# A decoder block on one core: x turned unscaled, its row factors applied at the PSUM copies, and the bias row's matmuls at the front

## The reference

```python
def rmsnorm(x, g):
    xf = x.astype(jnp.float32)
    y = xf * lax.rsqrt(jnp.mean(xf * xf, axis=-1, keepdims=True) + EPS)
    return (y * g.astype(jnp.float32)).astype(x.dtype)

h = rmsnorm(x, g_mix[layer])
proj = h @ w_in[layer]                       # (512, 1024) @ (1024, 5632)
q, k, v, u, gate_a, gate_s = jnp.split(proj, SPLITS, axis=-1)
attn = diff_attention(q, k, v, rel_bias, lam, subln_g[layer], lam_init)   # 8 heads, two softmaxes each, T5 bias
y = s5_ssm(u, ...)                           # 32 groups of 16 channels, 64 complex states
z_val, z_gate = jnp.split(jax.nn.gelu(y) @ w_glu[layer], 2, axis=-1)
mixed = jax.nn.sigmoid(gate_a) * attn + jax.nn.sigmoid(gate_s) * (z_val * jax.nn.sigmoid(z_gate))
x = x + mixed @ w_out[layer]
h = rmsnorm(x, g_mlp[layer])
x = x + jnp.square(jax.nn.relu(h @ w1[layer])) @ w2[layer]
return rmsnorm(x, g_final)
```

## Time and profile before

| | us |
|---|---|
| median of 3 timed runs | 774.8 |
| lowest, highest | 773.28, 776.76 |
| the profiled execution's own time | 769.86 |
| its span (first to last instruction) | 768.1 |
| TensorE busy in it | 747.2 (97%) |
| VectorE (DVE) busy | 529.9 (69%) |
| ScalarE (ACT) busy | 359.5 (47%) |
| GpSimd (POOL) busy | 29.2 (4%) |

### The profile page before, as it was taken

How to read it: one execution, slowest core, us unless ns; L and a number is a source line. 1 busy time by engine, 2 the same in 40 slices (tenths; PEclk the granted TensorE clock), 3 DMA queues, 4 the chain that set the end, 5 groups by cost and what they waited for, 6 DMA issues and landing times.

```text
span 768.1 us, 10026 instructions
## 1 busy us (share of the span) xinstructions
PE 747.2 (97%) x3754; PEld 611.2 (80%) x3754; DVE 529.9 (69%) x951; ACT 359.5 (47%) x630; POOL 29.2 (4%) x28
## 2 busy tenths in 40 slices
PE   6999999999999999999999999999999999999995
PEld 5878878777777777888878787888888888888884
DVE  4679998655556673436742578866886498748896
ACT  7524631255556663732322645533543345334454
POOL 2210000000000100000000000000000000000015
PEclk9999999999999999999999999999999999999998
DMA  7673429922223530236237131183108320743002
GB/s 245 195 164 117 103 94 183 219 72 70 69 69 108 168 110 2 84 108 247 83 110 192 55 101 37 52 225 108 55 1 231 126 83 0 191 139 91 19 2 109
DMA packets 91824, 85.21 MB, mean 111 GB/s; under 512 B 10028, under 2 KB 68064, under 8 KB 91776
## 3 DMA queue, kind: packets, MB, share of 16 engines
q1 hardware_dynamic: 90944, 82.85, 38.4%
q10 hardware_dynamic: 832, 1.71, 1.1%
HBM read 77.11 MB, written 5.34 MB: 107 GB/s over the span
## 4 chain that ended last, share of the span: by engine, by line
PE 75%; DVE 16%; ACT 3%; issue 3%; DMA 2%; SPq 1%; DVEq 0%; ACTq 0%
PE ps L1649 22%; PE ps L1651 22%; PE ps L1650 22%; PE ps L1940 3%; PE ps L1921 3%; DVE w_lo L1008 2%; DMA raw<-in_w_in 1%; PE ps L1930 1%; DMA mixA<-in_x 1%; PE ps L1724 1%; DVE w_lo L1412 1%; DVE fr L1425 1%; DVE rt L1257 1%; DVE mixA L1383 1%; ACT fa_hi L880 1%
## 5 line engine op out<-in xcount | busy, mean ns | idle before, releaser
L1649 PE MATMUL ps<-hT_hi,w_hi 128*128 128x512 f32 x384 | 152.6, 397 | 0.4 <-DVE hT_lo L980 0.3
L1651 PE MATMUL ps<-hT_hi,w_lo 128*128 128x512 f32 x384 | 150.1, 391 | 0.0
L1650 PE MATMUL ps<-hT_lo,w_hi 128*128 128x512 f32 x384 | 149.7, 390 | 0.0
L1649 PE MATMUL ps<-w_hi,hT_hi 128*128 128x512 f32 x288 | 114.3, 397 | 0.0
L1651 PE MATMUL ps<-w_hi,hT_lo 128*128 128x512 f32 x288 | 112.4, 390 | 0.0
L1650 PE MATMUL ps<-w_lo,hT_hi 128*128 128x512 f32 x288 | 112.3, 390 | 0.0
L847 ACT ACTIVATE w_hi<-raw 128x1024 fp32r<-128x1024 f32 x78 | 81.7, 1052 | 56.4 <-PE ps L1651 56.4
L1412 DVE TENSOR_TENSOR w_lo<-raw,w_hi 128x1024 fp32r<-128x1024 f32 x78 | 94.2, 1221 | 15.6 <-ACT w_hi L847 14.7
L613 ACT ACTIVATE w_hi<-raw 128x1024 fp32r<-128x1024 f32 x62 | 64.8, 1058 | 68.5 <-PE ps L1651 58.3
L1008 DVE TENSOR_TENSOR w_lo<-raw,w_hi 128x1024 fp32r<-128x1024 f32 x58 | 70.4, 1222 | 32.4 <-ACT w_hi L613 31.8
L1649 PE MATMUL ps<-w_hi,fa_hi 128*128 128x512 f32 x224 | 87.4, 390 | 1.4 <-DVE fa_lo L1435 1.2
(11 more groups left out here) (256 smaller groups left out, 996.0 us busy)
## 6 DMA issues: line engine op xcount, KB each, us to landing
raw<-in_w SPq DMA_DIRECT2D x64, 512.0 KB, 4.3
raw<-in_w_in SPq DMA_DIRECT2D x44, 512.0 KB, 5.1
raw<-in_w_glu SPq DMA_DIRECT2D x8, 512.0 KB, 3.9
raw<-in_w_out SPq DMA_DIRECT2D x8, 512.0 KB, 4.0
mixA<-in_x SPq DMA_DIRECT2D x4, 512.0 KB, 5.4
bias<-frow_dram SPq DMA_DIRECT2D x32, 64.0 KB, 2.0
toep<-taps_dram SPq DMA_DIRECT2D x8, 256.0 KB, 9.6
x<-in_x SPq DMA_DIRECT2D x4, 512.0 KB, 6.7
```

What stands on the lines that cost most here:

```text
L1649: nc.tensor.matmul(dst, a_hi, b_hi, start=start, stop=False)
L1650: nc.tensor.matmul(dst, a_hi, b_lo, start=False, stop=False)
L1651: return nc.tensor.matmul(dst, a_lo, b_hi, start=False, stop=stop)
```

## The change

- SP issues `rb` and `oneh` first of all; then row tiles 0 to 2 of x, weight unit 0, row tile 3, and units 1 to 3.
- TensorE does the two bias matmuls as its very first work, and DVE their copies. `bias_row` behind `turn_prm` is gone, and so are DVE's two copies behind `mag`.
- TensorE turns x as it lands, unscaled. Tile 3 comes last with all its eight blocks; column 7 of tiles 0 to 2 is turned before it.
- ACT squares tiles 0 and 1 before the split of unit 0, and tiles 2 and 3 after the last `turn_hi`; one root and one reciprocal serve all four tiles.
- `w_lo` of unit 0 moves from GpSimd to DVE, in two halves, around the first `turn_lo`. TensorE does the u unit 0 column by column (all four row tiles for k = 0, then for k = 1).
- The row factor (`rstd`) comes in where ACT copies u, V and the gates (as the activation's scale). For q and k the tokens lie along the free axis: SP writes the four columns of `rstd` to DRAM (four DMAs of 128 x 4 bytes, in front of the load of unit 4) and reads them back spread over all partitions (`rows0`, 128 x 512, behind the taps' store). `copy_qk` moves from ACT to DVE as a scalar_tensor_tensor with `rows0` as second operand.
- In DVE's program `copy_qk(0)` stands behind `gate_a(0)`, `copy_qk(1)` behind the w_lo of unit 22 and in front of `gate_a(1)`, and the others at the end of each pair.

```diff
@@ SP
-        for t in range(TOK):
+        sp.dma_start(rb[:, :], rel_bias).then_inc(onehot_in, 16)
+        sp.dma_start(oneh[:, :], onehot).then_inc(onehot_in, 16)
...
-        for u in range(RING):
+        for t in range(TOK - 1):
+            load_x(t)
+        load_raw(0)
+        load_x(TOK - 1)
+        for u in range(1, RING):
             load_raw(u)
...
+        sp.wait_ge(x_rstd, TOK)
+        for t in range(TOK):
+            sp.dma_start(rstd_dram[P * t:P * t + P].unsqueeze(1), rstd[:, 0, t:t + 1]).then_inc(rstd_out, 16)
+
+        def load_rows0():
+            sp.wait_ge(taps_mm, 1)
...
+            sp.dma_start(rows0[:, :], bass.AP(rstd_dram.tensor, 0, [[0, P], [1, SEQ]])).then_inc(rows0_in, 16)
@@ ACT
+        square_x(0)
+        square_x(1)
         act.wait_ge(cols_turned, 1)
...
         for k in range(KT):
             turn_hi(0, k, g1_col)
-            if k == 2:
+            if k == 3:
                 split_hi(1)
+        square_x(2)
+        square_x(3)
+        act.wait_ge(x_squared, TOK)
+        nc.scalar.activation(ms[:, 0, 1, :], ms[:, 0, 0, :], ACT.Sqrt, bias=eps_t[:, :],
+                             scale=1.0 / D_MODEL).then_inc(x_rt, TOK)
...
-                                             ACT.Identity).then_inc(nat_copied, 1)
+                                             ACT.Identity, scale=rstd[:, 0, t:t + 1]).then_inc(nat_copied, 1)
@@ DVE
+        dve.wait_ge(frow_mm, 1)
+        TS(frow[:, 0:512], ps[0:N_HEADS, 5, :], 1.0, None, ALU.mult).then_inc(frow_out, 1)
...
+        split_first(0)
         dve.wait_ge(cols_copied, 1)
-        for k in range(KT):
+        turn_lo(0, 0, g1_col)
+        split_first(1)
+        for k in range(1, KT):
             turn_lo(0, k, g1_col)
...
+        def copy_qk(v):
+            h = v // 2
+            if v == 0:
+                dve.wait_ge(states_done, 2)
+                dve.wait_ge(frow_done, 16)
+                dve.wait_ge(rows0_in, 16)
+            dve.wait_ge(unit_used, U_QK + v + 1)
+            if h >= 2:
+                dve.wait_ge(score_ready, TOK * (h - 1))
+            dst, src = (qT, kT)[v % 2][:, h % 2, :], ps[:, qk_bank(v), :]
+            STT(out=dst, in0=src, scalar=HEAD_DIM ** -0.5 if v % 2 == 0 else 1.0, in1=rows0[:, :],
+                op0=ALU.mult, op1=ALU.mult).then_inc(qk_copied, 1)
+
         split_lo_to(U_QK + 2)
         gate_a(0)
+        copy_qk(0)
         split_lo_to(U_QK + 3)
+        copy_qk(1)
         gate_a(1)
         split_lo_to(U_QK + 4)
...
             if i == 0 and h >= 1:
                 gate_o(h - 1)
+            if h < N_HEADS - 1:
+                copy_qk(2 * (h + 1) + i // 2)
@@ TensorE
+        pe.wait_ge(onehot_in, 32)
+        nc.tensor.matmul(ps[0:N_HEADS, 5, :], rb[:, :], oneh[:, 0:512], start=True, stop=True)
...
         for t in range(TOK):
-            pe.wait_ge(x_scaled, t + 1)
-            for k in range(KT - 1):
+            pe.wait_ge(x_in[t], 16)
+            for k in (0, 3, 4, 5, 6, 1, 2) if t == 0 else range(KT) if t == TOK - 1 else range(KT - 1):
...
+        for k in range(2):
+            if k:
+                pe.wait_ge(w_lo_done, 1)
+            else:
+                pe.wait_ge(w0_part, 1)
+            for t in range(TOK):
+                pe.wait_ge(hT_lo_done, max(t, k) + 1)
+                mm = drive_input(U_SSM, t, k)
+        unit_done(mm)
```

More of the change, by code:

```diff
@@ L177, in build @@
     y_sb = sb("y_sb", [P, CHUNK, PAIRS, SSM_GROUP], offset=at["CL"])
+    rows0 = sb("rows0", [P, SEQ], offset=at["CL"] + 16384)
     y_nat = sb("y_nat", [P, TOK, SSM_WIDTH], offset=at["u_nat"])
@@ L550, in _ @@
         nc.gpsimd.memset(powers[:, 0, 1, :], 0.0).then_inc(tiles_set, 1)
-        for u in range(U_V):
+        pool.wait_ge(w_lo_done, 1)
+        for u in range(1, U_V):
             pool.wait_ge(w_hi_done, u + 1)
@@ L595, in _, with square_x @@
             act.dma_start(dst, src).then_inc(cols_in, 16)
-        for t in range(TOK):
+        def square_x(t):
             act.wait_ge(x_in[t], 16)
@@ L982, in turn_lo, with split_first @@
             ins.then_inc(hT_lo_done, 1)
-        for t in range(TOK):
-            dve.wait_ge(x_rt, t + 1)
-            nc.vector.reciprocal(rstd[:, 0, t:t + 1], ms[:, 0, 1, t:t + 1]).then_inc(x_rstd, 1)
-            dve.wait_ge(x_rstd, t + 1)
-            TS(mixA[:, t, :], mixA[:, t, :], rstd[:, 0, t:t + 1], None, ALU.mult).then_inc(x_scaled, 1)
+        dve.wait_ge(frow_mm, 1)
+        TS(frow[:, 0:512], ps[0:N_HEADS, 5, :], 1.0, None, ALU.mult).then_inc(frow_out, 1)
+        TS(frow[:, 512:BIAS_W], ps[0:N_HEADS, 6, 0:BIAS_W - 512], 0.0, MASKED, ALU.mult, ALU.add).then_inc(frow_out, 1)
+        def split_first(half):
+            cs = slice(512 * half, 512 * half + 512)
+            dve.wait_ge(w_hi_done, 1)
+            TT(w_lo[:, 0, cs], raw[:, 0, cs], w_hi[:, 0, cs].bitcast(F32),
+               ALU.subtract).then_inc(w_lo_done if half else w0_part, 1)
+        split_first(0)
         dve.wait_ge(cols_copied, 1)
-        for k in range(KT):
+        turn_lo(0, 0, g1_col)
+        split_first(1)
+        for k in range(1, KT):
             turn_lo(0, k, g1_col)
+        dve.wait_ge(x_rt, TOK)
+        nc.vector.reciprocal(rstd[:, 0, :], ms[:, 0, 1, :]).then_inc(x_rstd, TOK - 1)
+        dve.wait_ge(x_rstd, TOK - 1)
+        TS(rstd[:, 1, :], rstd[:, 0, :], 0.5, None, ALU.mult).then_inc(x_rstd, 1)
         def prow(i):
@@ L1742, in _, with drive_input @@
                                     ident[0:2 * KT + UT, 0:2 * KT + UT]).then_inc(cols_turned, 1)
-        pe.wait_ge(cols_copied, 1)
-        for t in range(TOK):
-            mm = turn_x(t, KT - 1)
-        mm.then_inc(turned, 1)
-        for u in range(U_SSM, U_V):
+            if t == TOK - 2:
+                pe.wait_ge(cols_copied, 1)
+                for t0 in range(TOK - 1):
+                    turn_x(t0, KT - 1)
+        def drive_input(u, t, k):
+            tc_, wc = slice(P * t, P * t + P), slice(512 * (k % 2), 512 * (k % 2) + 512)
+            return mm3(ps[:, B_S + t, :], hT_hi[:, k, tc_], hT_lo[:, k, tc_], w_hi[:, u, wc], w_lo[:, u, wc],
+                       k == 0, k == KT - 1)
+        for k in range(2):
[7 more added lines that the diff above has]
+        unit_done(mm)
+        for u in range(U_SSM + 1, U_V):
             pe.wait_ge(w_lo_done, u + 1)
             for t in range(TOK):
-                if u == U_SSM:
-                    pe.wait_ge(hT_lo_done, t + 1)
                 for k in (2 * u, 2 * u + 1):
```

56 lines of the change are left out of this document (19 added, 37 removed).

## The result

The changed kernel takes 781.5 us in the median of 13 runs (778.8 to 784.4), the kernel before 774.8 in 13 runs beside it (768.8 to 776.8): ratio 1.0106, 95% interval 1.0084 to 1.0129, slower by 8.2 us by the ratio and 6.7 by the medians. The forecast was 774.1, range 771.3 to 777.0. The profiled execution spans 781.8 us, its own time is 783.58, its mean granted clock 0.987 (before: 768.1, 769.86 and 0.997).

The account below looks back on a forecast made before the run. TensorE's work (busy 747.2 of 768.1 us) plus its gaps was taken as the bound. Front 0.3 plus bias row 1.76 gave 2.1 us, cut at the first heads to about 0.65: 774.8 to about 774.1, range 771.3 to 777.0.

Parts of the forecast that it names:

- Steps 1 and 2: Front, x's landing to first matmuls: tile 3 lands near 11.65 us, matmul 1 at 13.75, matmul 4 at 15.0; 0.6 gained.
- Step 3: Clock in the front: a late rise to full clock loses 0.3 us, leaving 0.3 gained, between -1.0 and +0.9.
- Step 4: Cover in the front: later splits and four small writes ahead of unit 4's load stay hidden, cost 0.
- Step 5: Bias row moved to the front: DVE goes on 1.76 us sooner; 2.1 us gained at drive, stall of about 0.4 left.
- Step 6: First heads: gate_a(1) comes onto DVE's path, waits of about 0.7 and 2.2 us; 0.7 of 2.1 us gain left.
- Step 7: Other attention pairs: DVE's extra 0.61 to 0.69 us in each of 14 pairs costs 0, bounds 0 and 3.6 us.
- rival (a): Later attention pairs: DVE's longer queue stalls TensorE in each of 12 pairs, +3.6 us, 777.7 us; chance 0.1.

Follow-up runs that it names:

- 3: Kernel before plus only the four small row-factor writes (128 x 4 bytes each) in front of unit 4's load: 777.7 us, ratio 1.0056.
- 9: Kernel before with one more GpSimd wait, so the u_pairs copy begins behind VectorE's low half of unit 7: 777.4 us, ratio 1.005.
- 13: Kernel before with the u_pairs copy on ScalarE and the toep loads and turn_states moved behind the loads of units 22 and 23: 767.7 us, 0.9921.
- 7: Kernel before with only the bias row (its loads, two matmuls and copies) moved to the front: 775.6 us, ratio 1.0021.
- 4: Kernel before plus the same row-factor bytes as one write of 128 x 16 bytes: 774.6 us, ratio 0.9999.
- 5: Changed kernel with the small writes near 90 us and the bias row's store behind the copies of the turned u: 778.6 us, ratio 1.0061.
- 6: Changed kernel with late small writes, the bias row's store behind the turned-u copies, and both VectorE orders mended: 773.1 us, ratio 1.0005.
- 14: Changed kernel with only gate_a(1) put ahead of the first k copy on VectorE: 779.0 us, ratio 1.0085.
- 15: Changed kernel with only the last head's k copy put ahead of the last low half of its pair: 778.7 us, ratio 1.0084.
- 8: Changed kernel with only the bias row's store moved behind the copies of the turned u: 779.8 us, ratio 1.0086.
- 1: Changed kernel with only the four small writes moved behind the CL crossings, near 90 us: 780.6 us, ratio 1.0089.
- 2: Changed kernel with gate_a(1) ahead of the first k copy and the last head's k copy ahead of its pair's last low half: 775.9 us, 1.0031.
- 12: The kernel of 10 with the toep loads and turn_states moved behind the loads of units 22 and 23: 766.5 us, ratio 0.9907.
- 11: Kernel before with the u_pairs copy moved from GpSimd to ScalarE: 771.2 us, ratio 0.9975.
- 10: The kernel of 6 with the u_pairs copy moved from GpSimd to ScalarE: 772.2 us, ratio 0.9975.

## Why the prediction was wrong

**Steps 1 and 2** were right within 0.15 us in the profiled execution. **Step 3:** tile 3's turns ran at the full clock (eight in 1.09 us, against 0.22 each in the earlier trace rows) and the matmuls followed at 0.23. The Trainium skill's rule ("TensorE: Matmul & The Clock Gate", Part 4), by which the full clock doesn't engage for transposes, does not hold in this row. This is read from the spacing; the granted clock's column shows 1.00 in both fronts. Against the one profile of the kernel before the front gains 0.78 us at the fourth matmul and 0.60 at the 28th. But the slow turns of the earlier trace rows belong to an execution, not to the kernel: in 3, 9 and 13, whose fronts are the old one, the last eight turns go at 0.11 too. Over all profiles the 28th matmul stands at 19.4 to 20.7 us in the ten changed fronts (mean 20.3) and at 19.9 to 21.1 in the six old ones (20.5; 7 is neither). The front's gain is then some 0.2 us, under the scatter and near the 0.3 forecast, but by luck: the 0.3 us taken off for a clock still low weren't lost, since none of the ten changed fronts has a slow matmul, and what shrinks the gain is that the old front is often faster than its one profile showed.

**Step 4 is the first that failed,** on the cost of the four small writes. "Some 2 us on a load that has 4 us ... Even 3 us more would stay hidden: 0." SP's issuing was indeed 1.93 us. What I left out is how long the writes hold the transfers behind them: unit 4 took 12.4 us in place of 5.1, and between 24 and 28 us, where DMA had moved 307 GB/s, it moved 20. The step's own sentence from the Trainium skill ("DMA: Bandwidth & Descriptors", Specifications: read-modify-write under 512 B) pointed there, and I let it weigh nothing because no row had a price. (Whether that is the mechanism no run shows: the 16-byte pieces of 4 are under 512 B as well and cost nothing that can be seen.) An unpriced cost needed an upper bound from a row, say the 8 us of a landing, and then the question who waits for unit 4. Measured: 0.56% in the kernel before (experiment 3), nothing with the bytes in one write (4).

**The step that was missing** is the knock-on. I asked of each delay whether TensorE waits for it, and not which copy moves past which row of operations. `u_pairs` had 9.5 us of cover by its dates, but only 3.8 us until VectorE's dense row began (49.85 against 53.67), and 2.1 if one takes off the 1.7 us by which the copy itself had held VectorE back. At that edge 0.4 us, from 0.2 ahead (5) to 0.2 behind (6), costs 14. The kernel before shows the mechanism in one row of its trace, a 32-element operation of 1.87 us beside GpSimd's copy.

**Step 5** was right in its place (no wait at `drive` nor at the taps in the changed kernel, whose TensorE came late; 0.5 us in 7, forecast 0.4) and, up to attention, in its size (7: 1.77 us, forecast 1.76), but not in its worth at the end. "The states are 2.1 us earlier too, so unit 23's load is" is the sentence that failed: the last state operation was 1.5 us earlier, the load 0.12. SP took 4.81 us to issue the four state transfers, 3.39 before, behind the `toep` loads and unit 22's, and the load landed 0.9 us later than before.

**Step 6** was right: the two waits, their order and `gate_a(1)` on the path. Its price of 1.4 us measured 1.7 to 2.5 (14).

**Step 7** was right for the pairs in the middle, where no wait for Pm, qT or kT turned up, so rival (a) is refuted. It failed in the last one: the last head's k copy stands behind three low halves, where in the middle pairs it is one, and the one idle stretch for ScalarE's half is in front of it. 1.96 us with the clock at 0.57 behind it; 1.7 to 2.7 us at the end (15). I had read one pair and multiplied.

The terms don't add up singly, and that is a finding: removing the store (8), the writes (1) or both (5) gave back 1 to 3.5 us of the 8, the two orders (2) 5.8 by the ratio, and all of them together (6) ended level with the kernel before, with no gain. Below it by more than 0.5% came only the kernels with both the copy and the `toep` order cured, and that gain is nearly as large without the change (13). What the change is worth once its writes, its store and its two orders are cured (12 against 13) stays open between a gain of 4 us and a loss of 2. The scatter of the kernel before is explained in part: the profile of 4 has the late unit 23 in a long execution, and 11 narrows the scatter and 13 more (766.5 to 768.1), which fits both places. Why the `toep` loads are slow in some executions stays open.

## What to carry to other kernels

A copy on GpSimd that reads SBUF has its deadline where VectorE's next dense row of two-input operations begins, not where its reader stands. Give every small write an upper bound in time on its queue and follow who sits behind it, and prefer one write of many bytes per partition to several of four. When a saving vanishes, look for the next load on the same in-order queue: moving the loads that are read last behind those read first was worth more here than the change. And before a few tenths of a us are read from a stage, look at it in more than one execution: the old front's 28th matmul alone moved by 1.2 us.

## What the runs showed that I had not expected

- The lock-out spans a row of operations. A copy of 1.9 us was held for 13.6, 14.9 and 16.05 us over several VectorE operations, and got in only where one waits for its predecessor's result. The page of the Trainium skill named above speaks of one instruction and gives no such length.
- 512 pieces of 4 bytes delayed a load behind them by 6 to 7 us (11.5 us in 3, 12.4 in the changed kernel, against 5.1); 128 of 16 bytes did nothing visible (5.2).
- A store issued from 3.1 us ahead to 0.2 us behind the load of `u_nat` stretched its landing from 6.8 to 17.9 to 20.1 us (the changed kernel, 1, 2 and 3); 0.5 us behind it (7) it didn't. The mechanism wasn't followed.
- While the `toep` loads of 256 KB ran, DMA moved 138 to 150 GB/s in the profile of the kernel before, 116 to 120 in that of 7 and 104 to 105 in those of 4 and 10, whose `toep` loads are the same. Why stays open.
- ScalarE's copies out of PSUM took 0.69 us with a scale read from SBUF and 0.60 with none.
